# A hybrid S5/GLA diffusion layer on one core: adaLN additions placed elsewhere in FFN1's segments, another order of the loads before q, gate products and merge on PSUM, output factor at the eviction

## The reference

```python
ml = split(silu(c) @ ada_w + ada_b, 9)          # adaLN vectors, 9 groups of 1024; mc for the context
x   = ffn_sublayer(x,   ml[0..2], ...)           # FFN1: x + gate * 0.5 * (silu(h@w_gate) * (h@w_up)) @ w_down
ctx = ffn_sublayer(ctx, mc[0..2], ...)           # the same weights
h   = modulate(rms_norm(x, mix_norm), ml[3], ml[4])            # also for ctx
u, q, k, v, r, glr, ga, gb = split(h @ w_in)
ya = s5_branch(u)                                # diagonal complex scan both ways, gelu, GLU
yb = gla_branch(q, k, v, r, glr)                 # chunked gated linear attention both ways, group norm, * silu(r)
y  = (sigmoid(ga) * (ya @ s5_out) + sigmoid(gb) * (yb @ gla_out)) @ w_o
x  = x + ml[5] * y
x  = ffn_sublayer(x, ml[6..8], ...)              # FFN2, latent tokens alone
return rms_norm(x, final_norm)
```

## Time and profile before

| | |
|---|---|
| median of 3 runs | 1648.67 us (1648.06 to 1649.17) |
| the profiled execution | 1648.26 us |
| its span, first to last instruction | 1646.5 us |
| mean granted clock of PE | 0.933 of 2.4 GHz |
| busy: PE, DVE, POOL, ACT | 90%, 47%, 41%, 17% |
| chain that ended last | PE 75%, DVE 16%, nothing the profile shows 3%, ACT 3%, DMA 2% |

### The profile page before, as it was taken

The page is one execution under the profiler, slowest core; times in us unless marked ns, Lnnn a source line. Parts: engine busy times, 40 slices in busy tenths (PEclk is TensorE's granted clock), DMA queues, the critical chain, the costliest instruction groups (busy, mean ns, idle before and its releaser), DMA issues.

```text
span 1646.5 us, 18966 instructions
## 1 busy us (share of the span) xinstructions
PE 1488.7 (90%) x7868; PEld 1307.6 (79%) x7868; DVE 769.8 (47%) x1017; ACT 272.8 (17%) x423; POOL 679.0 (41%) x389
## 2 busy tenths in 40 slices
PE   6899999899899899969689999777797999999996
PEld 6899998798898899848578887655575888888885
DVE  5475556556445444461225997565835111121124
ACT  5220110110110110130022214642112000100102
POOL 1263345234234334411046570511343566565650
PEclk8699999899899999959799999798888999999997
DMA  9162353353353342124345354401432233333311
GB/s 344 32 174 67 113 143 95 94 139 91 99 135 94 115 119 77 43 78 127 99 131 147 97 153 125 144 26 37 160 88 71 81 112 93 98 95 93 100 52 51
DMA packets 231986, 174.29 MB, mean 106 GB/s; under 512 B 28600, under 2 KB 212060, under 8 KB 231900
## 3 DMA queue, kind: packets, MB, share of 16 engines
q1 hardware_dynamic: 210416, 138.30, 28.8%
q10 hardware_dynamic: 21484, 34.78, 6.6%
HBM read 155.26 MB, written 17.79 MB: 105 GB/s over the span
## 4 chain that ended last, share of the span: by engine, by line
PE 75%; DVE 16%; issue 3%; ACT 3%; DMA 2%; SPq 1%; ACTq 1%; POOL 0%; DVEq 0%; PEldq 0%; POOLq 0%
PE ps L751 48%; PE ps L898 13%; PE ps L901 4%; PE ps L760 2%; DVE xs L1936 2%; DVE xs L1934 2%; PE ps L823 2%; DVE st L1932 2%; DVE st L1930 1%; PE ps L792 1%; DVE ssq L1709 1%; DVE st L1931 1%; PE ps L814 1%; PE ps L988 1%; DVE h_lo L1752 1%
## 5 line engine op out<-in xcount | busy, mean ns | idle before, releaser
L680 POOL TENSOR_SCALAR w_hi<-w_raw 128x1024 fp32r<-128x1024 f32 (+2 forms) x187 | 217.5, 1163 | 891.0 <-issue 491.9
L683 POOL TENSOR_TENSOR w_lo<-w_raw,w_hi 128x1024 fp32r<-128x1024 f32 (+2 forms) x187 | 459.9, 2459 | 15.6
L751 PE MATMUL ps<-h_hi,w_lo 128*128 128x384 f32 (+2 forms) x1344 | 425.0, 365 | 31.0 <-POOL w_lo L683 19.7
L751 PE MATMUL ps<-h_lo,w_hi 128*128 128x384 f32 (+2 forms) x1344 | 419.5, 361 | 0.0
L751 PE MATMUL ps<-h_hi,w_hi 128*128 128x384 f32 (+2 forms) x1344 | 418.2, 360 | 0.0
L751 PEld LDWEIGHTS ps<-h_hi,w_lo 128*128 128x128 f32 (+1 forms) x1344 | 245.2, 191 | 63.3 <-POOL w_lo L683 25.2
L751 PEld LDWEIGHTS ps<-h_hi,w_hi 128*128 128x128 f32 (+1 forms) x1344 | 247.2, 190 | 24.6
L751 PEld LDWEIGHTS ps<-h_lo,w_hi 128*128 128x128 f32 (+1 forms) x1344 | 247.8, 191 | 23.5
L1793 DVE SCALAR_TENSOR_TENSOR ps<-ps,silu 128x768 f32<-128x768 f32 (+1 forms) x44 | 36.6, 832 | 317.0 <-PE ps L751 317.0
L1816 DVE SCALAR_TENSOR_TENSOR x<-ps,mod,x 128x512 f32<-128x512 f32 x96 | 70.6, 747 | 166.4 <-PE ps L901 88.9
L898 PE MATMUL ps<-act_hi,w_lo 128*128 128x512 f32 x352 | 140.0, 398 | 2.2 <-DVEq L1798 2.2
(11 more groups left out here) (300 smaller groups left out, 1741.5 us busy)
## 6 DMA issues: line engine op xcount, KB each, us to landing
w_raw<-in_ffn_w_gate_dram SPq DMA_DIRECT2D x44, 512.0 KB, 3.8
w_raw<-in_ffn_w_up_dram SPq DMA_DIRECT2D x44, 512.0 KB, 3.8
w_raw<-in_ffn_w_down_dram SPq DMA_DIRECT2D x40, 512.0 KB, 3.4
ada_w<-in_ada_w_dram ACTq DMA_DIRECT2D x32, 512.0 KB, 3.8
w_raw<-in_w_in_dram SPq DMA_DIRECT2D x32, 512.0 KB, 4.1
ada_w<-in_ada_w_dram SPq DMA_DIRECT2D x30, 512.0 KB, 5.2
c_scr<-cp ACTq DMA_DIRECT2D x16, 288.0 KB, 3.5
b_scr<-bt_sb ACTq DMA_DIRECT2D x16, 256.0 KB, 3.3
```

The source lines that it names most:

```text
L680: pool.tensor_scalar(w_hi[:, s, 0:cols], w_raw[:, s, 0:cols], 1.0, 1.0, ALU.mult, ALU.mult)\
L683: pool.tensor_tensor(w_lo[:, s, 0:cols], w_raw[:, s, 0:cols], w_hi[:, s, 0:cols].bitcast(F32), ALU.subtract).then_inc(w_split, 1)
L751: last = pe.matmul(mv[2], st, mv[part], start=(first and q == 0), stop=(n == len(terms) - 1 and q == 2))
```

## The change

- FFN1, segments 1 to 4: the additions stand behind the column tiles as (0), (1, 2), (3, 4), (5, 6), and tile 7 behind down job 3. Nothing stands behind down job 7. ACT's loads move along.
- Group 8 has the second accumulator (`ada_acc0`), and DVE's wait for `ada7` is gone. SP issues k's two loads and q's first ahead of the spill of x, q's second between groups 7 and 8, r's first two within group 8.
- The S5 output products are evicted by DVE, multiplied with the gate a (`take_ma` moves from ACT to DVE, behind the states). SP loads the gates: six tiles of a behind the GLU, two more when slots come free, four of b behind the last attention output, four more as they come free.
- The merge works in PSUM: mb times gate b in place, plus ma in place; ACT takes the high part from there and DVE the low part, and the slot is free only after that.
- The end: ACT writes `xg`, x times `final_norm`, k tile by k tile beside the squares; PE transposes `xg` (tiles 0 to 3 before the row sums, 4 to 7 after), without a spread of the reciprocal root; the factor of each token is applied at the eviction, half of a row tile by ACT and half by DVE. There are four output buffers and eight half stores. A Sqrt on one column stands ahead of the squares.
- The column sums of the adaLN groups stay attached to the same jobs.

```diff
@@ ada
+def ada_acc0(g):
+    return 1 if g > ADA_MIX else 0
@@ SP
+            tall(UNIT["k"], 2, C_K)
+            tall(UNIT["q"], 1, C_Q)
             sp.wait_ge(xn_ok, 2 * KD)
             sp.dma_start(x_scr, x[:, :, 0:NL]).then_inc(x_spilled, 16)
             for k in range(KD):
                 ada_tile(ADA_MIX, k)
-                if k in (3, 7):
-                    tall(UNIT["k"] + k // 4, 1, C_K + P * (k // 4))
+            tall(UNIT["q"] + 1, 1, C_Q + P)
             for k in range(KD):
                 ada_tile(ADA_MIX + 1, k)
-                if k in (3, 7):
-                    tall(UNIT["q"] + k // 4, 1, C_Q + P * (k // 4))
-            tall(UNIT["r"], 4, C_R)
+                if k in (3, 6):
+                    tall(UNIT["r"] + k // 4, 1, C_R + P * (k // 4))
+            tall(UNIT["r"] + 2, 2, C_R + 2 * P)
...
+                if name == "ma":
+                    is_done(sp, JOB["glu"] + 3)
+                    for c in range(2):
+                        sp.wait_ge(gate_out[c], 128)
+                    for t in range(6):
+                        load_gate_a(t)
+            for t in (6, 7):
+                was_read(sp, MA_JOB[t - 6])
+                load_gate_a(t)
+            is_done(sp, GJ["out", 3] + 3)
+            for t in range(4):
+                load_gate_b(t)
...
                 if q == 4:
+                    for t in range(4, KD):
+                        sp.wait_ge(gate_b_used, t - 3)
+                        load_gate_b(t)
                     is_done(sp, JOB["mb"] + KD - 1)
...
             for t in range(4):
-                sp.wait_ge(outc_ok, t + 1)
-                sp.dma_start(out[0, P * t:P * t + P, :], out_sb[:, t % 2, :]).then_inc(out_done[t % 2], 16)
+                for ready, c in ((out_low, slice(0, 512)), (out_high, slice(512, D))):
+                    sp.wait_ge(ready, t + 1)
+                    sp.dma_start(out[0, P * t:P * t + P, c], out_sb[:, t, c]).then_inc(out_done, 16)
@@ PE, end
-            norm_sum(JOB["norm3"], NL)
-            pe.wait_ge(fin_ok, KD)
+            for k in range(4):
+                pe.wait_ge(xg_ok, k + 1)
+                for t in range(4):
+                    transpose(ctx_(JOB["out"] + t)[:, P * k:P * k + P], xg[:, k, P * t:P * t + P])
+            row_sums(JOB["norm3"], NL)
...
@@ ACT
+                if q == 3:
+                    act.activation(oms[:, 0:1], eps[:, :], ACT.Sqrt)
                 for k in range(KD):
...
+                    if q == 3:
+                        act.activation(xg[:, k, :], x[:, k, 0:n], ACT.Copy, scale=vt[:, 96 + k:97 + k])\
+                            .then_inc(xg_ok, 1)
...
-                            for k in ((0, 1), (2,), (3,), (4,))[f]:
+                            for k in ((0, 1), (2,), (3, 4), (5, 6))[f]:
                                 ada_tile(g, k)
...
-                        for k in (5, 6, 7):
-                            ada_tile(g, k)
+                        ada_tile(g, KD - 1)
...
-                act.activation(m_hi[:, t, :], mt[:, t % 2, 2, :], ACT.Copy).then_inc(mh_ok, 1)
-                if t + 2 < KD:
-                    load_gates(t + 2)
+                act.activation(m_hi[:, t, :], lat(JOB["mb"] + t), ACT.Copy).then_inc(mh_ok, 1)
...
+                act.activation(out_sb[:, t, 0:512], ctx_(j), ACT.Copy, scale=root[:, t:t + 1]).then_inc(out_low, 1)
@@ DVE
                         if ada_here_now:
-                            ada_add(ADA_START + nth, f_)
+                            for e in ((0,), (1, 2), (3, 4), (5, 6))[f_]:
+                                ada_add(ADA_START + nth, e)
...
-                        if ada_here_now and k % 4 == 3:
-                            for e in (k + 1, k + 2) if k == 3 else (6, 7):
-                                ada_add(ADA_START + nth, e)
+                        if ada_here_now and k == 3:
+                            ada_add(ADA_START + nth, KD - 1)
...
-                    if k == 0 and g > ADA_MIX:
-                        is_done(dve, JOB["ada7"])
                     ada_add(g, k)
...
+            def take_ma(name, p):
+                for _ in range(MA_AFTER.get((name, p), 0)):
+                    t = taken_ma[0]
+                    j = MA_JOB[t]
+                    dve.wait_ge(gate_a_in[t % 6], 16 * (t // 6 + 1))
+                    is_done(dve, j)
+                    TT(ma[:, t, :], lat(j), gate_a(t), ALU.mult).then_inc(slot_read[j % 4], 1)
+                    taken_ma[0] += 1
...
                 dve.sem_inc(s_ok, 1)
+                take_ma("kv", p)
...
             def m_low(t):
                 dve.wait_ge(mh_ok, t + 1)
-                TT(m_lo[:, t, :], mt[:, t % 2, 2, :], m_hi[:, t, :].bitcast(F32), ALU.subtract).then_inc(m_ok, 1)
+                j = JOB["mb"] + t
+                TT(m_lo[:, t, :], lat(j), m_hi[:, t, :].bitcast(F32), ALU.subtract).then_inc(m_ok, 1)
+                dve.wait_ge(m_ok, t + 1)
+                dve.sem_inc(slot_read[j % 4], 1)
...
-                TT(mt[:, t % 2, 0, :], ma[:, t, :], gates[:, t % 2, 0, :], ALU.mult)
                 is_done(dve, jb)
-                TT(mt[:, t % 2, 1, :], lat(jb), gates[:, t % 2, 1, :], ALU.mult).then_inc(slot_read[jb % 4], 1)
-                was_read(dve, jb)
-                TT(mt[:, t % 2, 2, :], mt[:, t % 2, 0, :], mt[:, t % 2, 1, :], ALU.add).then_inc(m32_ok, 1)
+                TT(lat(jb), lat(jb), gate_b[:, t % 4, :], ALU.mult).then_inc(gate_b_used, 1)
                 if t:
                     m_low(t - 1)
+                dve.wait_ge(gate_b_used, t + 1)
+                TT(lat(jb), lat(jb), ma[:, t, :], ALU.add).then_inc(m32_ok, 1)
...
-            norm_root(JOB["norm3"], NL)
-            norm(3, NL)
+            was_read(dve, JOB["norm3"])
+            dve.reciprocal(root[:, 0:4], root[:, 0:4]).then_inc(rows_ok, 1)
+            dve.wait_ge(rows_ok, 1)
+            for t in range(4):
+                j = JOB["out"] + t
+                is_done(dve, j)
+                TS(out_sb[:, t, 512:D], lat(j), root[:, t:t + 1], None, ALU.mult).then_inc(out_high, 1)
```

93 lines of the change are left out of this document (40 added, 53 removed).

## The result

The changed kernel takes 1569.38 us (median of 4 runs, 1567.73 to 1574.98); the kernel before took 1648.92 us in runs on the same chip. The ratio is 0.9523, with a 95% interval of 0.9507 to 0.9539. The forecast was 1574.2 us, with a range of 1565 to 1589. The profiled execution took 1570.27 us with a span of 1568.5, so 78.0 us less span than before, where the sum of the prediction was 74.1.

What follows compares the result with a forecast made beforehand. TensorE, 90% busy, was taken to bound the kernel, so only its waits and slow stretches could be won. Gains 25.8 + 23.5 + 12.7 + 12.1 = 74.1 us off span 1646.5 give 1572.4, forecast 1574.2 us, range 1565 to 1589.

Steps and rivals of the forecast that it cites:

- Part 1: Heads of FFN1 segments 2 to 4: moved adaLN additions end PE's wait for s5_b; gain 25.8 us, bounds 22 to 27.
- the slower clock right after 32 of them: FFN1 heads: column sums stay at the same matmuls, so PE's slow clock behind 32 of them stays too; no gain counted.
- Rival B: FFN1 tiles: moved additions collide with GpSimd's weight splits, costing half the heads' gain; 1587 us, chance 8%.
- Part 2: k, q and adaLN groups 7 and 8: earlier loads and separate accumulators let PE run unbroken; gain 23.5 us, bounds 20 to 24.5.
- what follows moves as a whole: Behind ada8's sums: S5 stream loads, lam_p and the scan hang on ada8 and shift with it, keeping the 23.5 us.
- Part 3a: S5 output products evicted by DVE with the gate: later decays and waits lose 2.0 us, bounds 0 to 5.
- Part 3b: Merge: three 0.7 us DVE operations a tile let PE set the pace and w_o start earlier; gain 14.7 us, bounds 7 to 16.
- Rival A: Merge: operations with a PSUM operand also wait for GpSimd, so its 14.7 us are not gained; 1589 us, chance 6%.
- Part 4: Kernel end: no broadcast or scalings, 16 transposes instead of 32 after the row sums; gain 12.1 us, bounds 9.5 to 13.
- Rival C: Loads: second q or group 8 still waits for raw slot or adaLN ring, 23.5 us not gained; 1598 us, chance 5%.
- rival D: FFN1 tiles: colliding additions push DVE past the tile's 18 us, slower than before; 1652 us or more, chance 2%.
- 1565 and 1591: Whole kernel: the prediction's stated times in us with its bounds all at once; the forecast with its bounds got 78%.

Runs made afterwards that it cites:

- the changed kernel again: The changed kernel run once more, unaltered, beside three variants of its ends and heads: 1570.93 us, ratio 0.9528 to the kernel before.
- the first trace: Profiled execution of the changed kernel from its first runs, nothing altered: 1570.27 us, span 1568.5 us.
- the second trace: Second profiled execution of the same changed kernel, nothing altered: span 1568.0 us.
- the old additions: Changed kernel with FFN1's adaLN additions back where they stood before, tiles 6 and 7 behind the last down job: 1596.54 us, ratio 0.9684.
- the old merge: Changed kernel with the whole mixer of the kernel before put back (ScalarE eviction, late gate loads, four VectorE operations a tile): 1585.20 us, ratio 0.9617.
- the sum in SBUF: Changed kernel with the merged sum written to SBUF instead of back to PSUM, still three VectorE operations a tile: 1575.39 us, ratio 0.955.

## Why the prediction was right, point by point

**The time.** 1569.38 us measured, 1574.2 forecast, and the changed kernel again 1570.93. Undoing one part at a time costs, against 1570.2, 26.3 us for the additions, 23.4 for part 2, 15.0 for the mixer and 12.5 for the end. Together that is 77.2, where 78.7 lie between the two kernels (1648.9 - 1570.2). Each difference is known to some 2 to 4 us by its interval; within that the parts add up and don't lean on each other. The profiled execution gained 3.9 us more than the sum of the prediction (78.0 against 74.1): 4.2 more in part 1, most of it by the clock, and next to nothing in the rest.

**Part 1**, 25.8 predicted. The three heads give 8.73 + 10.15 + 7.59 = 26.5 (9.37, 9.37 and 9.35 us against 18.10, 19.52 and 16.94). The stage gained 30.0, and the term was too small by the remaining 3.5: the prediction let "the slower clock right after 32 of them" stay as it was. In the first trace it stayed at one head (415.15, 1.75 us) and was absent at the other (305.43, 8.52 us), where the segment's first tile went 16.55 to 13.40 us. That is not the work of the change: in the second trace the clock fell at both, and there the stage gained 645.19 - 618.50 = 26.7. The nine traces with the new additions and undivided sums reach the tail's second product at 636.0 on average, 27.5 us ahead of the kernel before. So some 26 to 28 us belong to the change, as the run with the old additions says, too, and the 30.0 of the first trace, above the prediction's bound of 27, is a lucky one. The cost of the moved additions was put at 1.75 us each, with 2.8 us of DVE's idle time left; they took 1.41, and 1.97 us were left behind a tile with other work as well. Rival B had no hold: in segments 1 to 4 PE waited for DVE nowhere. The margin was small, 0.16 us for s5_b at the first head (0.2 by the prediction).

**Part 2**, 23.5 predicted, 23.15 measured. Also the steps of it came as described: no gap from k to the sums of group 8, whose additions ended at 776.15, 8 us ahead of the sums (12 by the prediction). What was not seen is that the accumulator does it alone (22.7 of the 23 us); the late q load was a second wait behind the first. And the step "what follows moves as a whole" was a little off: in the first trace r's first product ran at the slower clock (7.09 us), which gave back 1.6; in the second it took 5.51.

**Part 3a**, 2.0 us lost by prediction. The profile shows one step of it: behind pass 0 the first operation of the next decays (`e1q`) starts 2.8 us behind the end of the states in both traces of the changed kernel, and 0.24 us behind it in the kernel before and in the one with the old merge. But no loss is left in sum. From the sums of group 8 to the merge the three traces with the old eviction took 321.2, 323.8 and 324.5 us, the eleven with the new one 320.9 to 327.8, with a mean of 323.4 against 323.2. An effect of 2 us can't be told from that spread, and it stays open. One thing that may have taken up a part: the next two S5 output products ran faster (5.73 us instead of 7.20).

**Part 3b**, 14.7 predicted, 15.3 measured and reproduced to 0.01 us by the old merge. The choice that carried it, 0.7 us for an operation with a PSUM operand beside GpSimd's split, from the earlier trace rows, was 0.68 to 0.70. Rival A is out. What this choice was worth by itself is another matter: with the sum in SBUF the low part took 1.1 us and the merge kept PE's pace.

**Part 4**, 12.1 predicted, 12.1 measured, with errors that cancel, so that the exact hit is luck. The start of the row sums was to come 0.75 us late and didn't (FFN2 took 361.98 us, before 362.07), and the path from there to the last eviction took 4.4 us instead of 5.5. The prediction priced 16 transposes at 3.69 us from a row at a granted clock of 0.50, with the evictions behind them; they ran at 1.00 in 1.95 us, and the evictions waited for the root alone. In the trace where they took 3.41 us, the path took 5.1. On the other side the end lies 5.2 us behind the last eviction and not 3.5: the price was taken from a kernel that stored one row of tiles at a time, where now 2.10 MB go out at once.

**The chances.** Rival C (the loads don't come free in time) and rival D (DVE overloaded in each tile) had no sign in the trace. The bounds of the parts, added up, don't give the "1565 and 1591" of the prediction: the largest gains, 27 + 24.5 + 16 + 13 = 80.5 us, end at 1567.8, the smallest, 22 + 20 + 7 - 5 + 9.5 = 53.5, at 1594.8. The range that was stated holds the measured time, and so would the right one. The low end of the range, 1565, is just below the fastest run of any variant here.

## What to carry to other kernels

Look for an instruction that one engine does ahead of what the critical engine waits for at a stage's head, and move it behind a wait that exists anyway; its value is the wait and the slow restart after it. When two things are late at the same place, undo them one at a time: the one that was late first may be all there is. Price a short row of matmuls at the clock that it will be granted, not at that of the row it is read from. And count the bytes of the last stores before counting their issues.

## What the runs showed of the hardware that was not expected

- The same program shows the granted clock falling in or right behind a row of 32 single-column matmuls in one execution and not in the next (304 to 310 us: 1.00 in the first trace, 0.72 in the second), though PE is counted busy throughout; each fall costs some 1.5 to 3 us. With the sums divided into rows of 16 it stayed at 1.00 from 140 to 146 us in all three traces, and at 1.00 behind the later heads of the two in which PE had not stood idle ahead of them.
- What a VectorE operation with two SBUF operands costs beside GpSimd depends on where they meet: begun 0.4 us into a `w_lo` of 2.71 us it took 2.89 us, begun 0.55 us before its end 1.10, and with GpSimd at rest 0.69. In both meetings it ended some 0.55 us behind GpSimd's operation.
- Stores of the output at the end ran at 381 GB/s in 256 KB pieces and at 406 in 512 KB pieces, 5.5 and 5.2 us for 2.10 MB.
- Sixteen transposes of 128x128 took 1.95 us at a granted clock of 1.00, 3.41 at 0.55 and 3.69 at 0.50.
